# A hybrid attention and state-space encoder: attention steps that take two query heads of both key groups

## The chip, the cores and the metric

The kernel runs on one NeuronCore of a Trainium2 chip. The metric is the device time of one execution in microseconds (us), from the first to the last instruction and the little around them. The core has a matmul engine (PE, with its weight loads shown apart as PEld), a vector engine (DVE), a scalar engine (ACT), GpSimd (POOL) and a queue engine (SP) which here only starts transfers. Each runs its own list of instructions in order and waits for the others by semaphores. PE writes to eight banks of accumulators (`ps`), from which DVE and ACT read.

## The reference

Two sequences of 256 positions and 1024 channels go through two layers. Each layer projects its input once and splits the columns between windowed attention and a two-way state-space scan; the results are joined by an output projection, and a gated MLP follows. The change touches the attention alone:

```
q: 8 heads of 64, k and v: 2 groups of 64; heads 0-3 use group 0, heads 4-7 group 1
sc    = q_blk . k * HEAD_DIM**-0.5              # per block of 128 queries
mask  = (|q_pos - k_pos| <= 128) & in range
m     = max(max(sc), sink[head])
p     = exp(sc - m)
probs = p / (sum(p) + exp(sink[head] - m))
out   = probs . v                                # (block, head, 64)
```

All is computed in fp32 or by splitting a number into a high and a low part. There are 4 query blocks of 128 (`t`, two per sequence) and 8 heads, so 32 pairs of block and head in a layer.

## The kernel before

Both sequences lie side by side as 512 columns. A projection ("unit") streams 512 KB of weights from memory into a ring of five buffers; ACT takes the high part (`whi`, L545), DVE the low part (`wlo`, L1068), and PE makes 24 products of 128x512 per unit (L749, L750, L751). Units 0 to 26 of a layer are the input projection.

The order of all work is written out by hand in `mixer_schedule` (line 102) as one list of steps; every engine walks through it and does its own share of each step. For unit n it has `G` (the projection, PE), `E` (its first read, ACT), `F` and `F2` (a convolution of five taps on DVE, L1177), `SILU` (ACT, then DVE L1184), `S` (the split of the weights four units ahead). Attention is woven in from unit 8 on, one attention step i with each unit: `AS` (scores, PE), `AM` (row maxima, DVE L1322 to L1325), `AX` (four exponentials, ACT L682), `AD` (denominators, DVE), `AN` (division, POOL L494), `AP` (eight transposes of the probabilities on PE, L1007, and a copy by ACT, L691), `AV` (values, PE L1016; the result's high part by ACT L696, its low part by DVE L1338). `AP` of step i comes one unit after its scores and `AV` two units after. Besides there are `T` (transposes for the scan, L916), `CB` (L924), `MV` (POOL L524), and from unit 17 on the steps of the scan, among them `SB` (L957, L961) and `SD` (L977).

There are eight attention steps i per layer. `ATTN` (line 85) says what each holds: block t and key group g, that is, four heads of one block. The keys and values of group 0 lie in rows 0 to 63 of their buffers, those of group 1 in rows 64 to 127; the query buffer `qk[:, j]` holds head j of group 0 in its upper half and head j of group 1 in its lower half. So a step works with one half of the rows:

- `AS` writes banks 2 and 3. For each bank: a mask (L993, one product of the whole array), then two score products (L997) of 64 rows, all from rows g*64 to g*64+63.
- `AV` writes rows g*64 to g*64+63 of one bank by two products of 64 columns x 512 (L1016), one per block of keys.

An fp32 product shows as two records of PE in the trace, each with its weight load; a product of operands declared fp32r (the masks, the projections) shows as one.

The waits that matter here: the scores of step i wait for the exponentials of step i-1 (`as_exp`); DVE's `AM` waits for the scores (`as_full`); the transposes wait for POOL's division (`as_norm`); projection n waits until the convolution of unit n-2 has read its bank (`conv_taps`). The steps `AA` (L894, L895) and `SD` (L977) of before already put out into the two halves of a bank's rows in turn.

Of the kernel before, what the change touches and what calls it, by code (L numbers as in the profile page):

```python
# [19 lines left out]
ALU = mybir.AluOpType  # L20
# [4 lines left out]
P = 128  # L25
DEPTH, D_MODEL, SEQ, NSEQ = 2, 1024, 256, 2
TOK = NSEQ * SEQ
BLK = 128
# [53 lines left out]
PAIRS = [(g, t) for g in range(2) for t in range(NBLK)]  # L82
PRODS = [(i, kind) for i in range(len(PAIRS)) for kind in ("fwd", "bwd", "off")]
CN_HEAD = CN["upper"][0]
ATTN = [(t, g) for t in range(NBLK) for g in range(2)]
A0 = 8
PROD_SLOTS = {17: [0], 18: [1, 2], 19: [3, 4, 5], 20: [6, 7, 8], 21: [9, 10, 11], 22: [12, 13, 14],
              23: [15, 16, 17], 24: [18, 19, 20], 25: [21, 22], 26: [23]}
# [90 lines left out]
def trunk(nc, x_in, units, pm_d, pf_d, cn_d, gb_d, h_d, y_d):  # L179
    ctx = ExitStack()  # L180
    with ctx:
# [173 lines left out]
        def aux_bank(key):  # L355
            return 6 + aux_use[key] % 2
# [181 lines left out]
        def _(act):  # L538
# [61 lines left out]
            for L in range(DEPTH):  # L600
                act.wait_ge(pm_loaded, L * 16 + 16)
                for what, i in SCHED:
# [38 lines left out]
                    elif what == "SP":  # L641
                        act.wait_ge(dt_abs, L + 1)
                        A(sp[:, 2, :], sp[:, 1, :], ACT.Exp, scale=-1.0).then_inc(dt_exp, 1)
                        A(neg_a[:], pmc("a_log"), ACT.Exp).then_inc(dt_exp, 1)
                        act.wait_ge(dt_floor, L + 1)
                        A(sp[:, 2, :], sp[:, 4, :], ACT.Ln).then_inc(dt_log, 1)
                    elif what == "SM":
                        wait_aux_full(act, L, ("AA", 0))
                        A(own_hi[:], ps[:, aux_bank(("AA", 0)), :], ACT.Copy).then_inc(own_high, 1)
                        wait_aux_full(act, L, ("AO", 0))  # L650
                        for d in range(2):
                            rows = slice(d * 64, d * 64 + 64)
                            src = ps[rows, aux_bank(("AO", 0)), :].rearrange("p (a b s) -> p a b s", b=2, s=P)[:, :, d, :]
                            A(off_hi[rows, :, :], src, ACT.Copy).then_inc(off_high, 1)
                    elif what == "T":
                        wait_aux_full(act, L, ("T", i))
                        A(xs_tm[:, :, (i - 4) * P:(i - 3) * P], ps[:, aux_bank(("T", i)), :].rearrange("p (t c) -> p t c", c=P),
                          ACT.Copy, scale=0.5).then_inc(t_evac, 1)
                    elif what == "VT":
                        wait_aux_full(act, L, ("VT", 0))  # L660
                        A(v_tm[:], ps[:, aux_bank(("VT", 0)), :].rearrange("p (t c) -> p t c", c=P),
                          ACT.Copy).then_inc(v_done, 1)
                    elif what == "SE":
                        i, kind = PRODS[i]
                        k = 3 * i + ("fwd", "bwd", "off").index(kind)
                        act.wait_ge(seg_full, L * 24 + k + 1)
                        if kind == "bwd":
                            if i >= 1:
                                act.wait_ge(w_sum, L * 8 + i)
                        elif i >= 2:  # L670
                            wait_aux_full(act, L, ("SD", i - 2))
                        dst = {"fwd": e_fwd[i % 2], "bwd": e_bwd, "off": e_off[i % 2]}[kind]
                        b0 = 2 + 2 * (k % 2)
                        A(dst[:].rearrange("p h q -> p (h q)"),  # L674
                          ps[:, b0:b0 + 2, :].rearrange("p b n -> p (b n)"), ACT.Exp).then_inc(exp_done, 1)
                    elif what == "AX":
                        act.wait_ge(as_max, L * 8 + i + 1)
                        if i >= 2:

                            wait_y_full(act, L, ("AP", i - 2, 1))  # L680
                        for j in range(QPK):
                            A(sc[i % 2][:, j, :], ps[:, 2 + j // 2, (j % 2) * SEQ:(j % 2 + 1) * SEQ], ACT.Exp, scale=SCALE,  # L682
                              bias=ast[:, i % 2, 1, j:j + 1], accum_out=ast[:, i % 2, 3, j:j + 1])
                        A(ast[:, i % 2, 4, :], ast[:, i % 2, 2, :], ACT.Exp).then_inc(as_exp, 1)
                    elif what == "AP":
                        wait_y_full(act, L, ("AP", i, 1))
                        if i >= 2:
                            wait_aux_full(act, L, ("AV", i - 2))

                        assert y_bank(("AP", i, 0)) == 4  # L690
                        A(p_t[i % 2][:], ps[:, 4:6, :], ACT.Copy).then_inc(pt_done, 1)  # L691
                    elif what == "AV":
                        t, g = ATTN[i]
                        rows = slice(g * HEAD, (g + 1) * HEAD)
                        wait_aux_full(act, L, ("AV", i))
                        A(ahi[rows, 0:QPK, t * BLK:(t + 1) * BLK],  # L696
                          ps[rows, aux_bank(("AV", i)), :].rearrange("p (j q) -> p j q", q=BLK),
                          ACT.Copy).then_inc(ah_done, 1)
                    elif what == "SQ":
                        act.wait_ge(gated, L * 8 + (4 if i < 4 else 8))  # L700
                        if i >= 4:

                            act.wait_ge(rms_pair, L * 4 + 3)
                        A(sqr[i % 4][:], zs[:, i, :], ACT.Square).then_inc(rms_sq, 1)
                    elif what == "RMS":
                        act.wait_ge(rms_mm, L + 1)
                        A(std[:], ps[:, aux_bank(("RS", 0)), :], ACT.Sqrt, bias=cst("eps")).then_inc(rms_std, 1)
                    elif what == "RN":
                        act.wait_ge(ssd_normed, L * CT + i + 1)
                        A(ahi[:, QPK + i, :], zs[:, i, :], ACT.Copy).then_inc(sh_done, 1)  # L710
# [33 lines left out]
        def _(pe):  # L744
# [85 lines left out]
            for L in range(DEPTH):  # L830
                for what, i in SCHED:
# [147 lines left out]
                                              start=own, stop=not own, skip_group_check=True)  # L979
                        last.then_inc(aux_full, 1)  # L980
                    elif what == "AS":
                        t, g = ATTN[i]
                        rows = slice(g * HEAD, (g + 1) * HEAD)
                        if i == 0:
                            pe.wait_ge(rope_done, L * 5 + 5)
                            pe.wait_ge(as_const, 3)
# [1 line left out]

                            pe.wait_ge(as_exp, L * 8 + i)
                        o = 1 - t % 2  # L990
                        for m in range(2):

                            mm(ps[:, 2 + m, :].rearrange("p (j k) -> p j k", k=SEQ)[:, :, o * P:(o + 1) * P], big_i[:],  # L993
                               cut[:, t % 2, :].unsqueeze(1).broadcast_to((P, 2, P)), start=True, stop=False,
                               skip_group_check=True)
                            for n in range(2):
                                last = mm(ps[:, 2 + m, n * SEQ:(n + 1) * SEQ],  # L997
                                          qk[rows, 2 * m + n, t * BLK:(t + 1) * BLK],
                                          qk[rows, 4, (t // 2) * SEQ:(t // 2 + 1) * SEQ], start=False, stop=True,
                                          skip_group_check=True)  # L1000
# [7 lines left out]
                                                           sc[i % 2][:, j, kt * P:(kt + 1) * P], ident)  # L1008
                            last.then_inc(y_full, 1)
                    elif what == "AV":  # L1010
                        t, g = ATTN[i]
                        pe.wait_ge(v_done, L + 1)
                        pe.wait_ge(pt_done, L * 8 + i + 1)
                        wait_aux_free(pe, L, (what, i))
                        for kt in range(2):
                            last = mm(ps[g * HEAD:(g + 1) * HEAD, aux_bank((what, i)), :],  # L1016
                                      v_tm[:, (t // 2) * 2 + kt, g * HEAD:(g + 1) * HEAD], p_t[i % 2][:, kt, :],
                                      start=(kt == 0), stop=(kt == 1))
                        last.then_inc(aux_full, 1)
                    elif what == "RS":  # L1020

# [39 lines left out]
        def _(dve):  # L1061
# [99 lines left out]
            for L in range(DEPTH):  # L1161
                dve.wait_ge(pm_loaded, L * 16 + 16)
                for what, i in SCHED:
# [151 lines left out]
                        V.scalar_tensor_tensor(out=z, in0=y, scalar=0.5, in1=z, op0=ALU.mult, op1=ALU.mult).then_inc(gated, 1)  # L1315
                    elif what == "AM":

                        t, g = ATTN[i]
                        dve.wait_ge(as_full, L * 8 + i + 1)
                        sink = pmc("sink", g * QPK, (g + 1) * QPK)  # L1320
                        top, minus, sink_in = (ast[:, i % 2, n, :] for n in range(3))
                        chain(V.tensor_reduce(top, ps[:, 2:4, :].rearrange("p b (j k) -> p (b j) k", k=SEQ), AX_X, ALU.max))  # L1322
                        chain(V.scalar_tensor_tensor(out=top, in0=top, scalar=SCALE, in1=sink, op0=ALU.mult, op1=ALU.max))
# [8 lines left out]
                        chain(V.tensor_tensor(den, ast[:, i % 2, 3, :], ast[:, i % 2, 4, :], ALU.add))  # L1332
                        V.reciprocal(den, den).then_inc(as_den, 1)
                    elif what == "AV":
                        t, g = ATTN[i]
                        rows = slice(g * HEAD, (g + 1) * HEAD)
                        dve.wait_ge(ah_done, L * 8 + i + 1)
                        V.tensor_tensor(alo[rows, 0:QPK, t * BLK:(t + 1) * BLK],  # L1338
                                        ps[rows, aux_bank((what, i)), :].rearrange("p (j q) -> p j q", q=BLK),
                                        f(ahi[rows, 0:QPK, t * BLK:(t + 1) * BLK]), ALU.subtract).then_inc(al_done, 1)  # L1340
                    elif what == "RMS":
                        dve.wait_ge(rms_std, L + 1)
                        chain(V.reciprocal(std[:], std[:]))
# [78 lines left out]
def lay_out(x_prompt, x_sample, ln_in_g, ln_in_b, w_in, attn_sink, ssd_conv_w, ssd_conv_b, ssd_a_log,  # L1422
# [23 lines left out]
    for i in range(DEPTH):  # L1446
# [15 lines left out]
        cbias = np.concatenate([ssd_conv_b[i][SSD_WIDTH:], ssd_conv_b[i][:SSD_WIDTH]])  # L1462
        pms.append(np.concatenate([
            cw.reshape(5, N_CONV, P).transpose(2, 1, 0).reshape(P, 5 * N_CONV), channels(cbias),
            channels(ssd_norm_g[i]), everywhere(attn_sink[i]), everywhere(ssd_a_log[i]),
            everywhere(ssd_dt_bias[i]), channels(np.repeat(ssd_d[i], HEAD))], axis=1))
        pfs.append(np.concatenate([
            ffn_conv_w[i].reshape(3, FT, P).transpose(2, 1, 0).reshape(P, 3 * FT), channels(ffn_conv_b[i]),
# [26 lines left out]
```

## Time and profile before

| | |
|---|---|
| median of 3 runs | 1448.69 us (1447.71 to 1449.17) |
| the profiled execution | 1446.43 us, its span 1444.6 us |
| mean granted clock of PE | 0.991 |
| busy, share of the span: PE | 1393.3 us, 96% |
| PE weight loads | 1112.7 us, 77% |
| DVE | 767.1 us, 53% |
| ACT | 564.5 us, 39% |
| POOL | 194.3 us, 13% |
| score products (L997), 128 records | 36.1 us busy |
| value products (L1016), 64 records | 30.9 us busy |
| masks of the scores (L993), 32 records | 10.6 us busy |

Times of instructions are durations, and successive matmuls overlap in them: what a matmul costs PE is the distance from its start to the start of the next one. A granted clock of 1.00 is 2.4 GHz, one of 0.50 is 1.2 GHz.

### The profile page before, as it was taken

How to read it: one execution, taken by the hardware profiler on the slowest of the kernel's cores; microseconds unless marked ns; L12 is line 12 of the kernel's file. 1: busy time of each engine (PE TensorE's matmuls, PEld its weight loads, DVE VectorE, ACT ScalarE, POOL GpSimd, SP SyncE). 2: the span in 40 equal slices, each digit the busy share in tenths (PEclk: the TensorE clock that was granted, in tenths of full speed). 3: DMA queues.
4: the chain of work that ended last, by engine and by line, in shares of the span. 5: the costliest groups of instructions: out<-in, count | busy, mean ns of one | idle time of the engine just before them, and what ended most of it. 6: DMA issues, size and time to landing. Idle time of an engine off the chain costs nothing.

```text
span 1444.6 us, 16237 instructions
## 1 busy us (share of the span) xinstructions
PE 1393.3 (96%) x6676; PEld 1112.7 (77%) x6676; DVE 767.1 (53%) x1008; ACT 564.5 (39%) x849; POOL 194.3 (13%) x111
## 2 busy tenths in 40 slices
PE   6999999999999999999989999899989999999997
PEld 5776777777888888888777767677878888888885
DVE  5666675665544444432266767665655444443224
ACT  5445544343533333311253454534344333332112
POOL 1012320133100000060020124001610000001400
PEclk8999999999999999999999999999999999999999
DMA  3421111142232333333233211111413333333332
GB/s 154 147 72 45 44 45 58 45 175 88 73 102 93 97 102 90 100 121 98 73 91 133 59 44 44 59 44 59 177 56 117 91 99 102 89 101 122 97 90 100
DMA packets 33209, 129.93 MB, mean 90 GB/s; under 512 B 3728, under 2 KB 3888, under 8 KB 31984
## 3 DMA queue, kind: packets, MB, share of 16 engines
q1 hardware_dynamic: 32976, 128.61, 27.9%
q8 instruction: 53, 0.87, 0.3%
q0 software_dynamic: 160, 0.29, 0.1%
q14 instruction: 20, 0.16, 0.0%
HBM read 122.60 MB, written 6.29 MB: 89 GB/s over the span
## 4 chain that ended last, share of the span: by engine, by line
PE 85%; ACT 6%; DVE 4%; issue 2%; DMA 1%; POOL 0%; DVEq 0%; ACTq 0%
PE ps L749 17%; PE ps L750 17%; PE ps L751 17%; PE ps L792 7%; PE ps L793 7%; PE ps L794 7%; PE ps L997 2%; PE ps L1016 2%; PE ps L977 2%; ACT junk L550 2%; DVE hb L1083 1%; PE ps L1007 1%; ACT whi L545 1%; ACT e_fwd L674 1%; DVE cv L1177 1%
## 5 line engine op out<-in xcount | busy, mean ns | idle before, releaser
L749 PE MATMUL ps<-hhi,whi 128*128 128x512 f32 (+1 forms) x1200 | 466.4, 389 | 16.3 <-DVE hlo L1114 15.3
L750 PE MATMUL ps<-hlo,whi 128*128 128x512 f32 (+1 forms) x1200 | 455.8, 380 | 0.0
L751 PE MATMUL ps<-hhi,wlo 128*128 128x512 f32 (+1 forms) x1200 | 455.7, 380 | 0.0
L1068 DVE TENSOR_TENSOR wlo<-raw,whi 128x1024 fp32r<-128x1024 f32 x210 | 274.4, 1307 | 266.8 <-ACT whi L545 266.7
L545 ACT ACTIVATE whi<-raw 128x1024 fp32r<-128x1024 f32 x210 | 221.3, 1054 | 240.4 <-DMA raw<-in_units 240.1
L749 PEld LDWEIGHTS ps<-hhi,whi 128*128 128x128 f32 x1200 | 228.0, 190 | 66.2 <-issue 16.8
L750 PEld LDWEIGHTS ps<-hlo,whi 128*128 128x128 f32 x1200 | 228.2, 190 | 42.6 <-issue 2.4
L751 PEld LDWEIGHTS ps<-hhi,wlo 128*128 128x128 f32 x1200 | 228.0, 190 | 42.6
L792 PE MATMUL ps<-whi,uhi 128*128 128x512 f32 x352 | 139.4, 396 | 0.0
L794 PE MATMUL ps<-wlo,uhi 128*128 128x512 f32 x352 | 139.2, 396 | 0.0
L793 PE MATMUL ps<-whi,ulo 128*128 128x512 f32 x352 | 139.2, 396 | 0.0
L1363 DVE SCALAR_TENSOR_TENSOR gcv<-ps,pf,gcv 128x510 f32<-128x510 f32 x44 | 33.0, 749 | 158.9 <-ACT gcv L721 158.9
L721 ACT ACTIVATE gcv<-ps,pf 128x512 f32<-128x512 f32 x44 | 34.2, 777 | 171.7 <-PE ps L751 171.7
L471 POOL TENSOR_TENSOR hb<-hb,gb 128x1024 f32<-128x1024 f32 x8 | 20.9, 2646 | 498.9 <-DMA gb<-in_gb 498.9
L792 PE MATMUL ps<-whi,ahi 128*128 128x512 f32 x192 | 77.7, 404 | 2.5 <-DVE wlo L1068 2.4
L794 PEld LDWEIGHTS ps<-wlo,uhi 128*128 128x128 f32 x352 | 66.2, 188 | 16.0
L792 PEld LDWEIGHTS ps<-whi,uhi 128*128 128x128 f32 x352 | 66.2, 188 | 15.9
L793 PEld LDWEIGHTS ps<-whi,ulo 128*128 128x128 f32 x352 | 66.2, 188 | 15.8
L793 PE MATMUL ps<-whi,alo 128*128 128x512 f32 x192 | 76.0, 396 | 0.0
L794 PE MATMUL ps<-wlo,ahi 128*128 128x512 f32 x192 | 75.9, 396 | 0.0
L1373 DVE TENSOR_TENSOR guf<-gsg,ps 128x512 f32<-128x512 f32 x44 | 30.2, 687 | 83.0 <-PE ps L751 82.4
L1177 DVE SCALAR_TENSOR_TENSOR cv<-ps,pm,cv 128x508 f32<-128x508 f32 (+1 forms) x96 | 71.4, 744 | 2.8
(168 smaller groups left out, 1466.6 us busy)
## 6 DMA issues: line engine op xcount, KB each, us to landing
raw<-in_units SPq DMA_DIRECT2D x210, 512.0 KB, 3.6
gb<-in_gb SPq DMA_DIRECT2D x5, 1024.0 KB, 5.7
h_kept<-hb SPq DMA_DIRECT2D x2, 2048.0 KB, 9.3
ha<-h_kept SPq DMA_DIRECT2D x2, 2048.0 KB, 10.6
hb<-in_x SPq DMA_DIRECT2D x4, 512.0 KB, 6.2
out_y<-hb SPq DMA_DIRECT2D x4, 512.0 KB, 2.6
cn<-in_cn SPq DMA_DIRECT2D x1, 585.5 KB, 9.7
pm<-in_pm POOLq DMA_DIRECT2D x2, 80.0 KB, 3.4
```

The lines of the kernel that those rows point to most:

```text
L545: A(whi[:, m % RING, :], raw[:, m % RING, :], ACT.Copy).then_inc(unit_hi, 1)
L721: A(gcv[:], ps[:, bank, :], ACT.Identity, scale=pf[:, k * 3 + w0 + 1:k * 3 + w0 + 2], bias=pf[:, k + v0:k + v0 + 1]).then_inc(glu_center, 1)
L749: mm(out, whi[:, slot, cols], xhi, start=start, stop=False)
L750: mm(out, whi[:, slot, cols], xlo, start=False, stop=False)
L751: return mm(out, wlo[:, slot, cols], xhi, start=False, stop=stop)
L792: mm(ps[:, bank, :], xhi[:, rows], whi[:, slot, cols], start=start, stop=False)
L793: mm(ps[:, bank, :], xlo[:, rows], whi[:, slot, cols], start=False, stop=False)
L794: return mm(ps[:, bank, :], xhi[:, rows], wlo[:, slot, cols], start=False, stop=stop)
L1068: V.tensor_tensor(wlo[:, m % RING, :], raw[:, m % RING, :], f(whi[:, m % RING, :]), ALU.subtract).then_inc(unit_split, 1)
L1177: V.scalar_tensor_tensor(out=dst[:, :, lo:hi], in0=src[:, :, lo + s:hi + s], scalar=pmc("conv_w", 5 * j + tap, 5 * j + tap + 1), in1=dst[: ...
L1363: V.scalar_tensor_tensor(out=dst[:, :, 1:SEQ], in0=src[:, :, 0:SEQ - 1], scalar=pf[:, k * 3 + w0:k * 3 + w0 + 1], in1=dst[:, :, 1:SEQ], op ...
L1373: V.tensor_tensor(guf[:], gsg[:], ps[:, bank + 1, :], ALU.mult).then_inc(glu_done, 1)
```

## The change

`ATTN` now pairs a block t with a number m of 0 or 1. A step holds heads 2m and 2m+1 of group 0 and heads 2m and 2m+1 of group 1 of one block: still four heads. Bank 2 takes group 0's two heads, bank 3 group 1's. In `AS` both masks come first, and then four score products, whose rows alternate between the upper and the lower half. In `AV` each of two blocks of keys gives one product per group, of 64 columns x 256, whose output alternates between the upper and the lower half of one bank. ACT's and DVE's reads of that bank (L696 and L1338 before) now take 128 partitions x 256 in place of 64 x 512. The sink logits are sorted to match.

```
-ATTN = [(t, g) for t in range(NBLK) for g in range(2)]
+ATTN = [(t, m) for t in range(NBLK) for m in range(2)]
...
                     elif what == "AS":
-                        for m in range(2):
+                        for g in range(2):
-                            mm(ps[:, 2 + m, :].rearrange(...)[:, :, o * P:(o + 1) * P], big_i[:], cut...)
+                            mm(ps[:, 2 + g, :].rearrange(...)[:, :, o * P:(o + 1) * P], big_i[:], cut...)
-                            for n in range(2):
-                                last = mm(ps[:, 2 + m, n * SEQ:(n + 1) * SEQ],
+                        for n in range(2):
+                            for g in range(2):
+                                rows = slice(g * HEAD, (g + 1) * HEAD)
+                                last = mm(ps[:, 2 + g, n * SEQ:(n + 1) * SEQ],
                                           qk[rows, 2 * m + n, t * BLK:(t + 1) * BLK],
                                           qk[rows, 4, (t // 2) * SEQ:(t // 2 + 1) * SEQ], start=False, stop=True,
                                           skip_group_check=True)
...
                     elif what == "AV":
                         for kt in range(2):
-                            last = mm(ps[g * HEAD:(g + 1) * HEAD, aux_bank((what, i)), :],
-                                      v_tm[:, (t // 2) * 2 + kt, g * HEAD:(g + 1) * HEAD], p_t[i % 2][:, kt, :],
-                                      start=(kt == 0), stop=(kt == 1))
+                            for g in range(2):
+                                last = mm(ps[g * HEAD:(g + 1) * HEAD, aux_bank((what, i)), 0:2 * BLK],
+                                          v_tm[:, (t // 2) * 2 + kt, g * HEAD:(g + 1) * HEAD],
+                                          p_t[i % 2][:, kt, g * 2 * BLK:(g + 1) * 2 * BLK],
+                                          start=(kt == 0), stop=(kt == 1), skip_group_check=True)
...
-                        A(ahi[rows, 0:QPK, t * BLK:(t + 1) * BLK],
-                          ps[rows, aux_bank(("AV", i)), :].rearrange("p (j q) -> p j q", q=BLK),
+                        A(ahi[:, 2 * m:2 * m + 2, t * BLK:(t + 1) * BLK],
+                          ps[:, aux_bank(("AV", i)), 0:2 * BLK].rearrange("p (j q) -> p j q", q=BLK),
...
-                        V.tensor_tensor(alo[rows, 0:QPK, t * BLK:(t + 1) * BLK],
+                        V.tensor_tensor(alo[:, 2 * m:2 * m + 2, t * BLK:(t + 1) * BLK],
...
-            channels(ssd_norm_g[i]), everywhere(attn_sink[i]), everywhere(ssd_a_log[i]),
+            channels(ssd_norm_g[i]), everywhere(attn_sink[i].reshape(2, 2, 2).transpose(1, 0, 2)), everywhere(ssd_a_log[i]),
```

PE's instructions in the third attention step of a layer, before: the last product of the projection, the scores, the values and the transposes of two earlier steps, and the next projection's first product (`p_t` is the transposed probabilities, `sc` the probabilities).

```order
L751 MATMUL ps<-hhi,wlo 128x512
L993 MATMUL ps<-cut,big_i 128x2x128
L997 MATMUL ps<-qk 128x256 x2
L993 MATMUL ps<-cut,big_i 128x2x128
L997 MATMUL ps<-qk 128x256 x2
L1016 MATMUL ps<-p_t_68,v_tm 64x512 x2
L1007 MATMUL ps<-cn,sc_67 128x128 x8
L749 MATMUL ps<-hhi,whi 128x512
```

The same place afterwards (line numbers of the changed kernel: L992 and L998 for L993 and L997, L1018 for L1016, L1008 for L1007).

```order
L751 MATMUL ps<-hhi,wlo 128x512
L992 MATMUL ps<-cut,big_i 128x2x128 x2
L998 MATMUL ps<-qk 128x256 x4
L1018 MATMUL ps<-p_t_68,v_tm 64x256 x4
L1008 MATMUL ps<-cn,sc_67 128x128 x8
L749 MATMUL ps<-hhi,whi 128x512
```

The masks have moved together in front of all score products, and two value products of 512 columns have become four of 256.

DVE's instructions of the same kind of step before, from the row maxima to the first denominator instruction:

```order
L1322 TENSOR_REDUCE ast<-ps 128x4
L1323 SCALAR_TENSOR_TENSOR ast<-ast,pm 128x4
L1324 TENSOR_SCALAR ast<-ast 128x4
L1325 TENSOR_TENSOR ast<-pm,ast 128x4
L1338 TENSOR_TENSOR alo<-ps,ahi 64x4x128
L1068 TENSOR_TENSOR wlo<-raw,whi 128x1024
L1177 SCALAR_TENSOR_TENSOR cv<-ps,pm,cv 128x2x254
L1177 SCALAR_TENSOR_TENSOR cv<-ps,pm,cv 128x2x255
L1332 TENSOR_TENSOR ast<-ast 128x4
```

And afterwards, where only the shape of the read of the values differs:

```order
L1325 TENSOR_REDUCE ast<-ps 128x4
L1326 SCALAR_TENSOR_TENSOR ast<-ast,pm 128x4
L1327 TENSOR_SCALAR ast<-ast 128x4
L1328 TENSOR_TENSOR ast<-pm,ast 128x4
L1340 TENSOR_TENSOR alo<-ps,ahi 128x2x128
L1071 TENSOR_TENSOR wlo<-raw,whi 128x1024
L1180 SCALAR_TENSOR_TENSOR cv<-ps,pm,cv 128x2x254
L1180 SCALAR_TENSOR_TENSOR cv<-ps,pm,cv 128x2x255
L1335 TENSOR_TENSOR ast<-ast 128x4
```

No instruction of DVE, ACT, POOL or SP has changed its place in its engine's list.

## Rows read from the trace of the kernel before

**Rows 1.** PE's waits: line, what it waited for, us, times, longest.

```profile
PE ps L749 <- DVE hlo L1114: 15.3, 9, 3.1
```

**Rows 2.** Busy time by engine, layers' attention stretches; then PE clock, DMA share, GB/s.

```profile
87.98:187.80 99.82, 99.68 (x430) 69.14 (x429) 69.29 (x120) 52.09 (x121) 30.22 (x18) 1.00 0.17 50
796.70:896.50 99.80, 99.65 (x430) 69.14 (x429) 69.28 (x120) 52.09 (x121) 30.21 (x18) 1.00 0.17 50
```

**Rows 3.** Time order, PE, first score step: start us, duration us, engine, line, operation.

```profile
87.98 0.28 PE L993 MATMUL ps<-cut,big_i 128*128 128x256 f32 x1
88.19 1.13 PE L997 MATMUL ps<-qk 64*128 64x256 f32 x4
...
88.51 0.81 PE L997 MATMUL ps<-qk 64*128 64x256 f32 x3
...
88.94 0.38 PE L997 MATMUL ps<-qk 64*128 64x256 f32 x1
89.25 0.38 PE L993 MATMUL ps<-cut,big_i 128*128 128x256 f32 x1
...
90.62 0.50 PE L749 MATMUL ps<-hhi,whi 128*128 128x512 f32 x1
```

**Rows 4.** Time order, PE, fp32r products of 256 columns.

```profile
33.55 0.28 PE L750 MATMUL ps<-hlo,whi 128*128 128x256 f32 x1
33.67 0.28 PE L751 MATMUL ps<-hhi,wlo 128*128 128x256 f32 x1
```

**Rows 5.** Time order, PE, first value step.

```profile
107.86 1.93 PE L1016 MATMUL ps<-p_t,v_tm 128*64 128x512 f32 x4
...
109.20 0.59 PE L1016 MATMUL ps<-p_t,v_tm 128*64 128x512 f32 x1
...
109.72 1.09 PE L1007 MATMUL ps<-cn,sc 128*128 128x128 f32 x8
```

**Rows 6.** Time order, PE, a state step that alternates column halves.

```profile
207.77 0.44 PE L977 MATMUL ps<-e_fwd,xs_tm 128*64 128x128 f32 x4 [0.20 <-DVE e_off L1296]
...
209.32 0.42 PE L977 MATMUL ps<-e_off,xs_tm 128*64 128x128 f32 x4
```

**Rows 7.** Time order, PE, cumulative sums; four records of L895 stand between.

```profile
54.08 0.44 PE L894 MATMUL ps<-cn,la_sides 128*64 128x128 f32 x4
...
54.51 0.44 PE L894 MATMUL ps<-cn,la_sides 128*64 128x128 f32 x4
```

**Rows 8.** Time order, DVE, POOL and PE, first three attention steps.

```profile
89.65 0.69 DVE L1184 SCALAR_TENSOR_TENSOR bc<-bc,cv 128x512 f32<-128x512 f32 x1 [0.70 <-ACT bc L640]
90.72 1.23 DVE L1322 TENSOR_REDUCE ast<-ps 128x4 f32<-128x1024 f32 x1 [0.38 <-PE ps L997]
...
97.54 0.69 DVE L1184 SCALAR_TENSOR_TENSOR bc<-bc,cv 128x512 f32<-128x512 f32 x1 [0.69 <-ACT bc L640]
...
95.56 1.89 POOL L494 TENSOR_TENSOR sc<-sc,ast 128x1024 f32<-128x1024 f32 x1 [58.08 <-DVE ast L1333]
...
96.19 0.28 PE L993 MATMUL ps<-cut,big_i 128*128 128x256 f32 x1
98.82 1.09 PE L1007 MATMUL ps<-cn,sc 128*128 128x128 f32 x8
...
105.22 0.28 PE L993 MATMUL ps<-cut,big_i 128*128 128x256 f32 x1
...
116.11 0.28 PE L993 MATMUL ps<-cut,big_i 128*128 128x256 f32 x1
```

**Rows 9.** Time order, DVE and PE, towards the end of the stretch.

```profile
175.94 2.25 DVE L1184 SCALAR_TENSOR_TENSOR xsc<-xsc,cv 128x512 f32<-128x512 f32 x1
...
179.81 0.60 PE L916 MATMUL ps<-cn,xsc 128*128 128x128 f32 x4
```

**Rows 10.** Busy time by engine, before and in a stretch of low clock.

```profile
355.00:359.40 4.40, 2.25 (x14) 1.64 (x13) 3.79 (x9) 1.95 (x4) 1.40 (x1) 1.00 0.67 236
359.50:362.80 3.30, 3.30 (x18) 3.30 (x17) 0.88 (x3) 3.27 (x8) 0.35 (x1) 0.50 0.00 0
```

More of the change, by code:

```diff
@@ L692, in _ @@
                     elif what == "AV":
-                        t, g = ATTN[i]
-                        rows = slice(g * HEAD, (g + 1) * HEAD)
+                        t, m = ATTN[i]
                         wait_aux_full(act, L, ("AV", i))
-                        A(ahi[rows, 0:QPK, t * BLK:(t + 1) * BLK],
-                          ps[rows, aux_bank(("AV", i)), :].rearrange("p (j q) -> p j q", q=BLK),
+                        A(ahi[:, 2 * m:2 * m + 2, t * BLK:(t + 1) * BLK],
+                          ps[:, aux_bank(("AV", i)), 0:2 * BLK].rearrange("p (j q) -> p j q", q=BLK),
                           ACT.Copy).then_inc(ah_done, 1)
@@ L981, in _ @@
                     elif what == "AS":
-                        t, g = ATTN[i]
-                        rows = slice(g * HEAD, (g + 1) * HEAD)
+                        t, m = ATTN[i]
                         if i == 0:
@@ L990, in _ @@
                         o = 1 - t % 2
-                        for m in range(2):
-                            mm(ps[:, 2 + m, :].rearrange("p (j k) -> p j k", k=SEQ)[:, :, o * P:(o + 1) * P], big_i[:],
+                        for g in range(2):
+                            mm(ps[:, 2 + g, :].rearrange("p (j k) -> p j k", k=SEQ)[:, :, o * P:(o + 1) * P], big_i[:],
                                cut[:, t % 2, :].unsqueeze(1).broadcast_to((P, 2, P)), start=True, stop=False,
                                skip_group_check=True)
-                            for n in range(2):
-                                last = mm(ps[:, 2 + m, n * SEQ:(n + 1) * SEQ],
+                        for n in range(2):
+                            for g in range(2):
+                                rows = slice(g * HEAD, (g + 1) * HEAD)
+                                last = mm(ps[:, 2 + g, n * SEQ:(n + 1) * SEQ],
                                           qk[rows, 2 * m + n, t * BLK:(t + 1) * BLK],
@@ L1010, in _ @@
                     elif what == "AV":
-                        t, g = ATTN[i]
+                        t, m = ATTN[i]
                         pe.wait_ge(v_done, L + 1)
@@ L1316, in _ @@
                     elif what == "AM":
-                        t, g = ATTN[i]
+                        t, m = ATTN[i]
                         dve.wait_ge(as_full, L * 8 + i + 1)
-                        sink = pmc("sink", g * QPK, (g + 1) * QPK)
+                        sink = pmc("sink", m * QPK, (m + 1) * QPK)
                         top, minus, sink_in = (ast[:, i % 2, n, :] for n in range(3))
@@ L1334, in _ @@
                     elif what == "AV":
-                        t, g = ATTN[i]
-                        rows = slice(g * HEAD, (g + 1) * HEAD)
+                        t, m = ATTN[i]
                         dve.wait_ge(ah_done, L * 8 + i + 1)
-                        V.tensor_tensor(alo[rows, 0:QPK, t * BLK:(t + 1) * BLK],
-                                        ps[rows, aux_bank((what, i)), :].rearrange("p (j q) -> p j q", q=BLK),
-                                        f(ahi[rows, 0:QPK, t * BLK:(t + 1) * BLK]), ALU.subtract).then_inc(al_done, 1)
+                        V.tensor_tensor(alo[:, 2 * m:2 * m + 2, t * BLK:(t + 1) * BLK],
+                                        ps[:, aux_bank((what, i)), 0:2 * BLK].rearrange("p (j q) -> p j q", q=BLK),
+                                        f(ahi[:, 2 * m:2 * m + 2, t * BLK:(t + 1) * BLK]), ALU.subtract).then_inc(al_done, 1)
                     elif what == "RMS":
```

## Prediction

> **What bounds the kernel now.** The first view is the list of what the matmul engine (PE) waited for. Its longest entry lies in the layer norms, 15.3 us [rows 1], and no line of the attention steps stands in it as a waiter. The second is the busy time in the two stretches that hold the attention steps, one per layer. PE is busy 99.68 of 99.82 us and 99.65 of 99.80 us at a granted clock of 1.00, the 2.4 GHz level; the vector engine (DVE) is busy 69.3 us, the scalar engine (ACT) 52.1 us and POOL 30.2 us [rows 2]. So PE sets the time there: what is taken from PE comes off the end, until one of the others is late. The third view is PE's instructions in order of time, which shows what one step costs PE.
>
> **Scores, before.** The steps of a score product are two masks (L993) and four products (L997). Each fp32 product stands as two records. From the first mask at 87.98 to the next projection at 90.62 the step takes 2.64 us [rows 3]. Inside it: mask to first score record 88.19 - 87.98 = 0.21. First to second record 88.51 - 88.19 = 0.32; then three records start from 88.51 to 88.94, so two gaps of 0.215, which I call a slot (256 columns of an fp32 product take two). Last record to the next mask 89.25 - 88.94 = 0.31. Two things are thus paid beside the slots. Going from a mask, which uses all 128 rows of the array, to a 64-row score, or back, costs about 0.1 us over what the instruction before it needs; and the first weight load behind such a change is open, 0.32 - 0.215 = 0.105. The step makes four such changes, the changed one makes two: both masks go first.
>
> **Scores, after.** Mask to mask costs one record of 256 columns in one pass, 33.67 - 33.55 = 0.12 [rows 4]. The four products become eight records, now four in the upper 64 rows and four in the lower. If the two halves run beside each other, each has four records: 0.12 + 0.21 + 0.32 + 2 x 0.215 + 0.31 = 1.39, and I add half a slot, 0.11, since the second half must load its weights behind the first. That makes 1.50 and saves 1.14 us a step. No row of before has two row halves in turn, so this is bounded from both sides. Low end: 1.39, no offset. If the halves run one after the other with their loads hidden, as now within one half, the eight records cost seven gaps: 0.12 + 0.21 + 0.32 + 6 x 0.215 + 0.31 = 2.25, saving 0.39. High end: every weight load open, 0.12 + 0.21 + 7 x 0.32 + 0.31 = 2.88, with the first one of the second half open as well 2.99, which would cost 0.35 more than now. I take 1.50, because the nearest rows, those of column halves below, show halves that run beside each other.
>
> **Values, before and after.** A value product (L1016) is two fp32 products of 512 columns, four records: 107.86 to the next engine use at 109.72 is 1.86 us [rows 5]. From the first start to the last is 109.20 - 107.86 = 1.34 = 0.05 + 3 x 0.43. Afterwards there are four products of 256 columns, of which two go to each column half. Here the trace has the answer: the state products (L977) write the two column halves in turn, and 28 records of 128 columns start between 207.77 and 209.32, 0.055 us each [rows 6]. A record of 128 columns alone takes half of the 0.215 that one of 256 takes [rows 3], 0.108. So alternating column halves double the rate, for fp32 too. The changed step is then 0.05 + 4 x 0.215 + (109.72 - 109.20 - 0.43 = 0.09) + 0.04 for an offset of the second half = 1.04, saving 0.82. Bounds: 0.86 without overheads, 1.86 if nothing overlaps.
>
> A second row tells how deep this overlap reaches. The cumulative sums of L894 and L895 are issued as L894, L895 for one column half, then L894, L895 for the other (lines 888 to 895). The trace groups them as four records of L894, then four of L895, the next four L894 0.43 us later [rows 7]: eight records of 128 columns in 0.43, and the other half's L894 has started before this half's L895. The halves run as two queues that do not wait for each other's order. The Trainium skill, "TensorE: Matmul & The Clock Gate" (What overlaps and what doesn't) says the opposite: matmuls start and end strictly in program order. By the skill's rule a half would have to wait for the second pass of the other; rows 7 speak against it. "TensorEngine Tiling (Array Packing)" of the Trainium skill (Key Properties) has tiles working independently of each other, and with that the trace agrees.
>
> **What becomes late.** The 16 steps of a layer's stretch (eight of scores, eight of values) save PE 8 x 1.14 + 8 x 0.82 = 15.7 us. DVE issues the same number of instructions in the same order; only L1338 and ACT's L696 change shape, from 64 partitions x 512 to 128 x 256, which cannot be longer, so I count nothing. DVE stays at 69.3 us of what would be 99.8 - 15.7 = 84.1, 82%. Its own load shows in the first step: from one silu (L1184) at 89.65 to the next at 97.54 are 7.89 us, of which 0.38 is a wait for the scores (L1322 at 90.72, its releaser L997): it needs 7.5. PE's first step now takes 96.19 - 87.98 = 8.21 and would take 7.07; the second 105.22 - 96.19 = 9.03, then 7.89; the third 116.11 - 105.22 = 10.89, then 8.94 [rows 8]. Only the first is shorter than DVE's. What is late is the first transpose of the probabilities (L1007 at 98.82). It needs POOL's product L494, 95.56 + 1.89 = 97.45, behind the reduction L1322. That one can only come forward to the end of the silu, 89.65 + 0.69 = 90.34, by 0.32 with the usual gap. So the product is ready at 97.13, while PE comes 2 x 1.14 earlier, at 96.54: 0.6 us of new wait. The same at the other end of the stretch: a silu that now takes 2.25 us beside POOL's work ends at 175.94 + 2.25 = 178.19, and PE transposes its result at 179.81 [rows 9]. The slack is 1.62, the two value steps in front of it give PE 1.62, and DVE gets part of that itself; I allow 0.3. Loss per layer 0.9.
>
> After the stretch PE's waits hang on chains that start with it and move with it: the state stage, the output projection, the loads (at most one of 512 KB per projection, as elsewhere), and POOL's affine work behind the reload. I let the gain through whole.
>
> **The sum.** Per layer 15.7 - 0.9 = 14.8, two layers 29.6 us. The profiled execution took 1446.43 us (span 1444.6 and 1.8 around it): 1416.8. The median of the runs stands 2.26 above it, so the forecast is 1448.69 - 29.6 = 1419.1 us.
>
> **Rivals.**
> 1. *Row halves do not overlap* (only the changes of mode are saved). For it: no row shows two row halves. Against: column halves do it, in fp32. Per layer 8 x 0.39 + 8 x 0.82 = 9.7, less 0.1: 19.2 us in all, 1429.5. Chance 0.13.
> 2. *Halves overlap only in program order*, so that the two records of a product stay behind each other and eight records take five slots instead of four. Against: rows 7. Scores 1.39 + 0.215 = 1.61, values 1.00 + 0.215 = 1.22, together 0.29 a step less, 16 times 4.6: 1423.7. The Trainium skill's rule on program order, named above, is this case. Chance 0.07.
> 3. *DVE and its chain become the bound* beyond the first step: each of the first four steps of a layer costs 1 us more than I count, as its waits for ACT (0.7 at each silu, [rows 8]) stop being covered. 8 us: 1427. Against: from the second step on PE's step is the longer one. Chance 0.06.
> 4. *Each row change opens a weight load*: scores 2.99 us, 0.35 x 16 = 5.6 dearer, values 13.1 cheaper, no new wait. 1441.2. Chance 0.04.
> 5. *Slower than before: the clock.* If PE's new waits in the attention steps bring its clock to 1.2 GHz, work there takes twice as long, so T us at the low level cost T/2. The trace has the low level at 359.5 to 362.8, granted 0.50, behind a stretch in which PE was busy 2.25 of 4.40 us [rows 10]. Slower needs 2 x 29.6 = 59 us of the 170 us of both stretches at that level; all of it would cost 85 us, 1504. Against: the waits I find are 0.6 and 0.3 us. Chance 0.03.
>
> **How the numbers follow.** The forecast has 0.67. Its own range is 1414 to 1424: the offset and the losses are worth 2 us either way, and a stretch of low clock in a layer norm (3.4 us, costing 1.7) may come or go as the work shifts, twice. The whole range reaches to rival 1 and over 2 and 3: 1413 to 1431, leaving out 4 and 5 and a bit of each. Changes under 0.2% (2.9 us) can't be told from none. Faster 0.96 (forecast and rivals 1 to 4), same 0.01, slower 0.03.
>
> **What would show it.** Right: the scores' records of the two halves start in pairs within one slot, first mask to next projection near 1.5 us; value steps near 1.04; attention stretches of 84 to 86 us with PE still over 98% busy; a wait of PE before the first transposes in each layer, released by POOL, near 0.6 us; the state stage as long as before. Wrong: score records at even gaps of 0.215 (rival 1) or five slots (2); PE waits of 1 us and more for DVE in many steps (3); gaps of 0.32 (4); granted clock under 1.00 in the stretches (5).

## The result, and the profile after

| | before | changed |
|---|---|---|
| median | 1448.21 us (4 runs, 1447.71 to 1449.17) | 1413.72 us (4 runs, 1412.00 to 1414.69) |
| ratio | | 0.976, 95% interval 0.9748 to 0.9772 |
| span of the profiled execution | 1444.6 us | 1410.2 us |

The change takes 34.5 us; 29.6 were forecast. The median lies inside the forecast's range of 1413 to 1431 us by only 0.7 us, and 0.3 us below the narrower range of its main case, 1414 to 1424.

The two attention stretches, as in [rows 2], in the same columns: span, busy time of PE, weight loads, DVE, ACT and POOL, granted clock.

```profile
87.95:171.01 83.06, 82.44 (x462) 64.03 (x460) 66.89 (x120) 50.28 (x121) 29.18 (x17) 1.00 0.20 58
779.20:862.20 83.00, 82.39 (x462) 64.02 (x460) 66.84 (x120) 50.28 (x121) 29.18 (x18) 1.00 0.20 58
```

Each stretch is 16.8 us shorter, PE is still busy in 99% of it at a granted clock of 1.00, and DVE now in 81%.

The first score step in PE's order of time, the counterpart of [rows 3]. The second fence is the same view cut to 50 ns: it keeps only the records that run in that moment.

```profile
87.95 0.39 PE L992 MATMUL ps<-cut,big_i 128*128 128x256 f32 x2
88.28 1.13 PE L998 MATMUL ps<-qk 64*128 64x256 f32 x8
89.34 0.50 PE L749 MATMUL ps<-hhi,whi 128*128 128x512 f32 x1
```

```profile
88.28 0.49 PE L998 MATMUL ps<-qk 64*128 64x256 f32 x2
```

Eight score records take the 1.13 us in which four stood before. Two records of 0.48 us begin at 88.28 and end together 0.49 us later: they start within 0.01 us of each other. The trace doesn't name the half of a record, but in the one-half kernel e3 below successive records start 0.215 us apart or more, so these two lie in different halves. The step is 89.34 - 87.95 = 1.39 us instead of 2.64, and it is that in 14 of 16 steps; the other two, one per layer, hold the wait below. The value step, counterpart of [rows 5]:

```profile
104.80 1.08 PE L1018 MATMUL ps<-p_t,v_tm 128*64 128x256 f32 x8
105.82 1.09 PE L1008 MATMUL ps<-cn,sc 128*128 128x128 f32 x8
```

It takes 1.02 us instead of 1.86. In the list of PE's waits one line is new, the first one below:

```profile
PE ps L1008 <- POOL sc L495: 1.2, 2, 0.6
...
PE ps L916 <- DVE xsc L1187: 0.4, 2, 0.2
```

The second has become smaller. Before, it was

```profile
PE ps L916 <- DVE xsc L1184: 1.3, 2, 0.7
```

Going through PE's groups of both traces one by one, from start to start, accounts for the rest. Per layer: eight score steps 8 x 1.25 = 10.0 us; eight value steps 8 x 0.85 = 6.8; the second score step holds a wait, -0.69; from L916 to L924 it is four times 0.16 less, 0.64; PE's wait before L916 in unit 18 is 0.65 before and 0.20 now, 0.45. That is 17.15 a layer and 34.3 in both, where the spans differ by 34.4. The groups between keep their length to 0.05 us, except in the layer norms: there single groups are up to 1.4 us longer or shorter, and these differences cancel to 0.1 us. Two profiles of the one changed kernel (after and a1) differ there in the same way, and by 1.6 us in one group of a state stage, so differences of this kind are not the change's.

### The profile page after: what moved, and what is told of

Its sections match the earlier page's. It is cut to its first block, busy times and chain, and to the rows that moved or that the text cites. A ratio compares the mean times of both kernels' runs of the same rounds, so it can differ in the third digit from the quotient of the medians.

```text
span 1410.2 us, 16365 instructions
## 1 busy us (share of the span) xinstructions
PE 1359.8 (96%) x6740; PEld 1103.2 (78%) x6740; DVE 757.5 (54%) x1008; ACT 560.0 (40%) x849; POOL 194.3 (14%) x111
## 4 chain that ended last, share of the span: by engine, by line
PE 83%; ACT 6%; DVE 6%; issue 3%; DMA 1%; POOL 1%; DVEq 0%; ACTq 0%; POOLq 0%
PE ps L749 17%; PE ps L751 17%; PE ps L750 17%; PE ps L792 8%; PE ps L793 7%; PE ps L794 7%; PE ps L977 2%; ACT junk L551 2%; DVE cv L1180 1%; DVE hb L1086 1%; PE ps L1008 1%; PE ps L1018 1%; ACT whi L546 1%; DVE wlo L1071 1%; ACT e_fwd L675 1%
## 5 line engine op out<-in xcount | busy, mean ns | idle before, releaser
L1071 DVE TENSOR_TENSOR wlo<-raw,whi 128x1024 fp32r<-128x1024 f32 x210 | 269.8, 1285 | 269.6 <-ACT whi L546 269.3
```

The costliest lines, as they stand in the source:

```text
L1071: V.tensor_tensor(wlo[:, m % RING, :], raw[:, m % RING, :], f(whi[:, m % RING, :]), ALU.subtract).then_inc(unit_split, 1)
```

## The experiments

Times are medians; the kernel before took 1448.13 us (1446.28 to 1449.22) beside e1, e3, e4 and e5, 1446.18 us (1445.4 to 1447.34) beside e2, e6 and e7, and 1447.86 us (1445.81 to 1449.47) beside e8, a1 and a2. The ratio to it is what compares across the groups. "Step" is the time from the first record of a score or value step to the next group of PE, as most of the 16 steps have it. e3 leaves out group 1's own queries and keys, e8 leaves out the second half of the array's columns, so neither computes group 1's attention.

| kernel | median us | ratio (95%) | score step | value step |
|---|---|---|---|---|
| e1, scores in blocks | 1411.97 | 0.9758 (0.9743 to 0.9772) | 1.39 | 1.02 |
| e2, values in blocks | 1412.90 | 0.9769 (0.9753 to 0.9786) | 1.39 | 1.02 |
| e3, one row half | 1425.09 | 0.9845 (0.9830 to 0.9860) | 2.25 | 1.02 |
| e4, before with masks first | 1441.74 | 0.9954 (0.9938 to 0.9971) | 2.25 | 1.86 |
| e5, masks between | 1430.89 | 0.9884 (0.9870 to 0.9899) | 2.64 | 1.02 |
| e6, reads by halves | 1418.09 | 0.9805 (0.9790 to 0.9820) | 1.39 | 1.02 |
| e7, division in two | 1411.79 | 0.9762 (0.9748 to 0.9777) | 1.39 | 1.02 |
| e8, one column half | 1425.51 | 0.9846 (0.9833 to 0.9860) | 1.39 | 1.87 |
| a1, changed kernel again | 1413.26 | 0.9760 (0.9746 to 0.9773) | 1.39 | 1.02 |
| a2, division in two again | 1412.77 | 0.9763 (0.9750 to 0.9776) | 1.39 | 1.02 |

### Does the overlap of row halves carry the score step? (e3, e8)

```
-                                rows = slice(g * HEAD, (g + 1) * HEAD)
+                                rows = slice(0, HEAD)
                                 last = mm(ps[:, 2 + g, n * SEQ:(n + 1) * SEQ],
```

> The changed kernel, but all four score products read the upper 64 rows (group 0's queries and keys), so the scores of group 1 are computed from the wrong operands; everything else stays. It takes the overlap of row halves away and leaves both masks first. If the overlap is what made the score step 1.39 us: step 1.39 + 4 x 0.215 = 2.25 us, +13.8 us in 16 steps, of which the wait of 0.69 us before the first transposes of each layer is given back: 1426. If fewer changes of mode explain the step: no change, 1413.7.

```profile
87.91 0.39 PE L992 MATMUL ps<-cut,big_i 128*128 128x256 f32 x2
88.23 1.99 PE L998 MATMUL ps<-qk 64*128 64x256 f32 x8
90.15 0.50 PE L749 MATMUL ps<-hhi,whi 128*128 128x512 f32 x1
```

In this order of time of e3 the same eight records take 1.99 us in one half where two halves need 1.13, and the step is 90.15 - 87.91 = 2.24 (2.25 in the table is the same by rounding). The wait before L1008 is gone from PE's list. The span is 1422.5 us, 12.3 above the changed kernel's; 16 x 0.86 - 2 x 0.69 = 12.4. The overlap theory holds, its rival (no change) falls. Row halves overlap fully, and that is worth 12.3 us, 13.7 in the steps less the 1.4 of the wait that it brings.

The same for the values:

```
-                                last = mm(ps[g * HEAD:(g + 1) * HEAD, aux_bank((what, i)), 0:2 * BLK],
+                                last = mm(ps[0:HEAD, aux_bank((what, i)), g * 2 * BLK:(g + 1) * 2 * BLK],
```

> The changed kernel, but all four value products go to the upper 64 columns of the array (group 1's result beside group 0's in the same rows of the bank), so that the reads take stale numbers for group 1; everything else stays. It takes the overlap of column halves away. If that overlap is the whole gain of the value step: 1.02 + 4 x 0.215 = 1.88 us a step, nothing given back, +13.8 us, about 1427.5. If shorter products of 256 columns explain part of it: less than 1.8 us a step.

```profile
104.80 1.94 PE L1018 MATMUL ps<-p_t,v_tm 128*64 128x256 f32 x8
106.67 1.09 PE L1008 MATMUL ps<-cn,sc 128*128 128x128 f32 x8
```

The value step is 106.67 - 104.80 = 1.87 us, what it was before with half as many products of twice the columns. So nothing of its gain comes from the shape of the products. The time is 1425.5 where about 1427.5 was expected. The steps give the expected 16 x 0.86 = 13.7; the span is 12.3 longer. 0.9 of the rest is read off the groups behind it: L916 to L924 became 0.04 us shorter and L924 to the next projection 0.07, eight times. In the changed kernel L924 starts as soon as its bank is free (see e6), and its second record starts 0.29 us after its first; in e8 PE comes later, the bank has been free for 0.42 us, and the second record follows after 0.22. So the wait for the bank still costs the changed kernel 0.11 us each time, 0.07 of it behind the wait. The layer norms, 0.7 us shorter in this profile, are the other part.

### Is it the alternation? (e1, e2)

The prediction called the halves two queues, from [rows 7]. These two kernels take the alternation away and leave the halves.

```
-                        for n in range(2):
-                            for g in range(2):
+                        for g in range(2):
+                            for n in range(2):
                                 rows = slice(g * HEAD, (g + 1) * HEAD)
```

> The changed kernel with the four score products in another order: both of group 0 first, then both of group 1, so that the row halves no longer alternate from product to product. If each half is a queue of its own, as the step of 1.39 us after the change suggests, the order doesn't matter: score step 1.39 us, time as the changed kernel, 1413.7 us. If halves overlap only in program order (the rule that matmuls start and end in order), just the last pass of group 0 lies beside the first of group 1: 7 slots of 0.215 instead of 4, step 2.04 us, 16 steps +10 us, 1424.

e2 has the same swap of loops, kt and g, in the value step.

> The changed kernel with the four value products in another order: both blocks of keys for group 0, then both for group 1. Independent column halves: value step 1.02 us as now, 1413.7 us. Overlap in program order only: 7 slots instead of 4, 1.66 us, 16 steps +10 us, 1424.

e1's score step, and then the same view cut to 150 ns at its start:

```profile
88.04 0.39 PE L992 MATMUL ps<-cut,big_i 128*128 128x256 f32 x2
88.36 1.14 PE L998 MATMUL ps<-qk 64*128 64x256 f32 x8
89.44 0.50 PE L749 MATMUL ps<-hhi,whi 128*128 128x512 f32 x1
```

```profile
88.36 0.49 PE L998 MATMUL ps<-qk 64*128 64x256 f32 x2
```

Two records start 0.01 us apart here too, so the first record of group 1 starts beside the first of group 0, although three other records of group 0 are issued ahead of it, and the step is 1.40 us. e2's value step is 1.02 us:

```profile
105.71 1.09 PE L1018 MATMUL ps<-p_t,v_tm 128*64 128x256 f32 x8
106.73 0.44 PE L1008 MATMUL ps<-cn,sc 128*128 128x128 f32 x2
```

Both times are that of the changed kernel within their intervals. Program order, which would have given steps of 2.04 and 1.66 us, is out. Both halves must merely be in one step; which comes first doesn't matter. In all these runs both halves hold the same amount of work, so that the record issued last also starts last; a step with unequal halves was not run. That speaks against the Trainium skill's sentence in "TensorE: Matmul & The Clock Gate" (What overlaps and what doesn't), that matmuls begin and end in program order; the rule of "TensorEngine Tiling (Array Packing)" (Key Properties), that tiles run independently, is what these runs show.

### What do the masks' places cost? (e4, e5)

e4 is the kernel before with the two masks in a loop of their own ahead of the products; e5 is the changed kernel with its masks back between them.

```
 e4:                    for m in range(2):
                            mm(ps[:, 2 + m, :]..., big_i[:], cut[...], start=True, stop=False, ...)
+                       for m in range(2):
                            for n in range(2):
                                last = mm(ps[:, 2 + m, ...], qk[rows, ...], qk[rows, 4, ...], ...)
 e5:                    for g in range(2):
                            mm(ps[:, 2 + g, :]..., big_i[:], cut[...], start=True, stop=False, ...)
-                       for n in range(2):
-                           for g in range(2):
+                           for n in range(2):
                                last = mm(ps[:, 2 + g, ...], qk[rows, ...], qk[rows, 4, ...], ...)
```

> The kernel before, with nothing changed but that both masks of a score step come ahead of its four products; groups and halves as before. Two of four changes between the whole array and 64 rows go: score step 2.64 - 0.39 = 2.25 us, 16 steps -6.2 us, 1442. If changes of mode cost nothing and only overlap pays: 1448.2.

> The changed kernel with the mask of bank 3 put back between group 0's two products and group 1's two, as the order of before was: mask, two, mask, two. If a product of the whole array between them drains both halves, nothing overlaps: score step 2.64 us as before, +20 us, less 1.4 for the first waits: 1432. If the halves could overlap across the mask: some 2.0 us a step, 1422.

e4's first score step, then e5's, in PE's order of time:

```profile
88.04 0.39 PE L992 MATMUL ps<-cut,big_i 128*128 128x256 f32 x2
88.36 1.99 PE L997 MATMUL ps<-qk 64*128 64x256 f32 x8
90.28 0.50 PE L749 MATMUL ps<-hhi,whi 128*128 128x512 f32 x1
```

```profile
87.93 0.28 PE L991 MATMUL ps<-cut,big_i 128*128 128x256 f32 x1
88.14 1.13 PE L996 MATMUL ps<-qk 64*128 64x256 f32 x4
89.19 0.38 PE L991 MATMUL ps<-cut,big_i 128*128 128x256 f32 x1
89.51 1.13 PE L996 MATMUL ps<-qk 64*128 64x256 f32 x4
90.57 0.50 PE L749 MATMUL ps<-hhi,whi 128*128 128x512 f32 x1
```

e4's step is 2.24 us, e5's 2.64, both as computed. e4 took 1441.7 us, 6.4 less than the kernel before, and 16 x 0.39 is 6.3: moving the masks is worth that much of the 34.5 by itself. In e5 the four records before the second mask are all in one half and the four behind it in the other; the mask needs all rows, and nothing passes it. e5 has both halves in one step, as the changed kernel, and gains nothing in its score step. So grouping both halves pays only for what stands on one side of a product of the whole array.

### Are the reads behind the values on PE's path? (e6)

In the result, two groups of PE that the change doesn't touch were shorter. My new theory: ACT's and DVE's reads of the values' bank are shorter (their forms in the traces: 0.59 and 0.68 us before, 0.38 and 0.42 now), and L924 waits for that bank.

```
-  A(ahi[:, 2 * m:2 * m + 2, ...], ps[:, aux_bank(("AV", i)), 0:2 * BLK]..., ACT.Copy).then_inc(ah_done, 1)
+  for g in range(2):
+      rows = slice(g * HEAD, (g + 1) * HEAD)
+      last = A(ahi[rows, 2 * m:2 * m + 2, ...], ps[rows, aux_bank(("AV", i)), 0:2 * BLK]..., ACT.Copy)
+  last.then_inc(ah_done, 1)
...                                   # DVE's subtraction in the same way
```

> The changed kernel, in which ACT and DVE read the values' bank in two instructions of 64 partitions x 256 each instead of one of 128 x 256. ACT's read then takes about 0.8 us instead of 0.38, DVE's 0.84 instead of 0.42. Theory: the shorter reads are on PE's path, since the products of L924 wait for the bank's release (al_done): four times per layer +0.8 us, and about 0.6 us once per layer in unit 18, where transposes wait for a chain behind these reads: +7.6 us, 1421. If the reads are covered, as I had counted: 1413.7.

PE and the reads in the fifth step's unit, first of the kernel before, then of the changed kernel, then of e6; DVE's read is the one that writes `alo`:

```profile
132.24 0.68 DVE L1338 TENSOR_TENSOR alo<-ps,ahi 64x512 fp32r<-64x512 f32 x1 [0.66 <-ACT ahi L696]
...
132.43 0.60 PE L916 MATMUL ps<-cn,xsc 128*128 128x128 f32 x4
133.06 1.10 PE L924 MATMUL ps<-bc 128*128 128x256 f32 x4
```

```profile
123.53 0.38 ACT L696 ACTIVATE ahi<-ps 128x256 fp32r<-128x256 f32 x1 [1.54 <-PE ps L1018]
...
124.26 0.42 DVE L1340 TENSOR_TENSOR alo<-ps,ahi 128x256 fp32r<-128x256 f32 x1
...
124.35 0.60 PE L916 MATMUL ps<-cn,xsc 128*128 128x128 f32 x4
124.82 1.10 PE L924 MATMUL ps<-bc 128*128 128x256 f32 x4
```

```profile
123.32 0.77 ACT L698 ACTIVATE ahi<-ps 64x256 fp32r<-64x256 f32 x2 [1.07 <-PE ps L1020]
...
124.12 0.86 DVE L1344 TENSOR_TENSOR alo<-ps,ahi 64x256 fp32r<-64x256 f32 x2
...
124.13 0.60 PE L918 MATMUL ps<-cn,xsc 128*128 128x128 f32 x4
125.12 1.10 PE L926 MATMUL ps<-bc 128*128 128x256 f32 x4 [0.39 <-DVE alo L1344]
```

From L916 to L924 are 0.63 us before, 0.47 in the changed kernel and 0.99 in e6. Before, DVE's read ends at 132.92 and L924 starts 0.14 later; the changed kernel's ends at 124.68, e6's at 124.98, and the product (L926 there) starts 0.14 and 0.15 later. The same distance, so this wait is on the path in all three. The waits before L916's transposes grew as well: PE's list of e6 has

```profile
PE ps L926 <- DVE alo L1344: 3.1, 8, 0.4
...
PE ps L918 <- DVE xsc L1189: 1.9, 4, 0.5
```

where the changed kernel has 0.4 us in two waits. Two of the four are those of unit 18, 0.5 where 0.2 was; the other two, 0.4 each, follow the layer's last value step, where the changed kernel has none. The theory holds: the reads are not covered. Its price was a little too high: by the ratios, 0.9805 - 0.9760 = 0.0045, it is 6.5 us where 7.6 were expected, and by PE's groups 8 x 0.51 + 2 x 0.31 + 2 x 0.51 = 5.7 (the median itself, 1418.1, was taken beside a kernel before that was 2 us faster there). Of the reads' 0.8 us more, only 0.52 arrives at L924. DVE's own 0.44 arrives whole. Of ACT's 0.39 only 0.08 does: in the changed kernel ACT's read ends at 123.91 and DVE, busy with its row maxima, starts its own at 124.26; in e6 ACT's ends at 124.09 and DVE's starts at 124.12.

### Can the new wait go? (e7, a1, a2)

```
-  nc.gpsimd.tensor_tensor(sc[i % 2][:], sc[i % 2][:], ast[...]..., ALU.mult).then_inc(as_norm, 1)
+  for kt in range(2):
+      part = sc[i % 2][:, :, kt * P:(kt + 1) * P]
+      nc.gpsimd.tensor_tensor(part, part, ast[...]..., ALU.mult).then_inc(as_norm, 1)
...
+  pe.wait_ge(as_norm, 2 * (L * 8 + i) + kt + 1)      # per key block in AP
```

> The changed kernel with POOL's division (L495) split into two instructions by key block, so that the first four transposes can start after the first half. Theory: the wait of PE for POOL before the first transposes (0.6 us, two times) goes, since the first half is ready some 0.95 us earlier and the second before the fourth transpose ends: -1.2 us, 1412.5. Rival: two instructions of 512 cost POOL clearly more than one of 1024 (1.9 us), and the second half comes later than the whole did: no gain or up to 1 us more.

The first transposes of the changed kernel and POOL's division, then both in a2, the same kernel as e7:

```profile
97.00 1.09 PE L1008 MATMUL ps<-cn,sc 128*128 128x128 f32 x8 [0.62 <-POOL sc L495]
...
95.05 1.89 POOL L495 TENSOR_TENSOR sc<-sc,ast 128x1024 f32<-128x1024 f32 x1 [57.61 <-DVE ast L1336]
```

```profile
96.30 0.66 PE L1009 MATMUL ps<-cn,sc 128*128 128x128 f32 x4
97.14 0.66 PE L1009 MATMUL ps<-cn,sc 128*128 128x128 f32 x4 [0.18 <-POOL sc L497]
...
95.05 2.04 POOL L497 TENSOR_TENSOR sc<-sc,ast 128x512 f32<-128x512 f32 x2 [57.61 <-DVE ast L1337]
```

The first four transposes start 0.70 us earlier, the other four wait for the second half, and two instructions cost POOL 0.15 us more than one. All eight take 1.25 us instead of 0.85, so the next projection starts at 97.55 instead of 97.85: 0.3 us won per layer, 0.6 in all, half of the 1.2 expected, because the second half comes later than the whole did (97.09 against 96.94), as the rival had it. The layer's last value step then takes 1.15 us instead of 1.02, and the wait in unit 18 is 0.13 shorter. e7 and the changed kernel had not run side by side, so both ran again on one chip.

> The changed kernel again, for the comparison with the split division on one chip: ratio 0.976 of the kernel before, two waits for POOL of 0.6 us.

> The changed kernel with POOL's division in two again, on the same chip as the changed kernel. Its first profile had a wait of 0.2 us where the changed kernel has 0.6 (twice); if nothing else hangs on it, 0.6 us (0.04%) less than the changed kernel, which the times can hardly tell from none; what the profiles differ in otherwise is the clock in the layer norms.

The ratios are 0.9760 (0.9746 to 0.9773) and 0.9763 (0.9750 to 0.9776). The profiles show the wait gone down, 1.3 to 0.4 us, and the times cannot tell the kernels apart. No version here is known to beat the changed kernel.

## Why the prediction was right, and where its terms were off

**What bounds the kernel** was right. PE was busy throughout the stretches and all that it gave up came off the end: 34.3 us by groups, 34.4 by the spans, 34.5 by the medians. The stretches are 83.1 us where 84 to 86 were named. Nothing became the bound behind it; DVE rose to 81% where 82% was worked out, though its busy time was held at 69.3 us and fell to 66.9. The gain was forecast a seventh too small, and the time is in the range by little: four of the five terms below were off in the same direction.

**Masks first**: 0.39 us a step, and 0.39 in e4.

**Row halves** ran beside each other as the nearest rows of column halves had suggested, and e3 shows it. The term was mis-sized by the half slot of 0.11 us that I added for the second half's weight load. The two first records start within 0.01 us, the step is 1.39, the low end of my bound: 16 x 0.11 = 1.8 us.

**Column halves**: 1.02 us for 1.04. The step fell by 0.85 where 0.82 was forecast, 0.5 us in all.

**The first wait**: 0.6 us forecast; PE waits 0.62 and the step is 0.69 longer, -0.2 us in all. Its place and its releaser, POOL's division, were right, and e7 moved it by splitting that instruction.

**The reads** were the step that failed: "which cannot be longer, so I count nothing". They became shorter, and e6 shows that PE waits for them. In [rows 2] and the list of waits this could not be seen: before, L924 started 0.63 us after L916 where 0.44 is enough (e8), and these 0.2 us stood in no line, being inside the overlap of matmul durations. It gave 8 x 0.16 = 1.3 us.

**The end of the stretch** went the other way: I allowed a loss of 0.3 us a layer before the transposes at 179.81 of [rows 9], and none came; in the changed kernel the silu ends 1.05 us before their counterpart starts. Instead PE gained 0.45 us a layer behind the stretch, in unit 18, where I had let the waits move along unchanged. The two make 1.5 us. This wait stood in the list of before, in the line of 1.3 us above. It ends a chain behind the last value step: ACT's read, its split of the next weights, DVE's part of the split, the convolution, the silu. ACT's read, first in the chain, is 0.21 us shorter; the split starts 0.1 us before the read has ended where it had started 0.02 behind it, which is 0.13 more, and the convolution 0.1 earlier in the same way. e6, which lengthens the reads, gives 0.31 back. Why the two later instructions start earlier was not taken apart.

The five sum to 1.8 + 0.5 - 0.2 + 1.3 + 1.5 = 4.9, the distance from 29.6 to 34.5, to the tenth or two that the rounding and the layer norms leave open. The time itself came out 5.4 us under 1419.1; the other 0.5 is the median of the kernel before, 1448.69 us in the forecast and 1448.21 beside the result.

**The rivals**: that row halves don't overlap falls by the 1.39 us step and by e3; overlap in program order by e1 and e2; DVE as the bound by the even steps of 1.39 and 1.02 us after the second; open weight loads and a low clock by the same steps and the granted 1.00 in both stretches.

## What to carry to other kernels

A product that fills half of the array's rows or columns leaves the other half free, and if the step before the next full product holds equal work for both halves, its products take half the time, in fp32 as well; the order within the step is of no account (e1, e2), but what stands on either side of a product of the whole array (here a mask) doesn't overlap (e5). Each change between the whole array and a half cost about 0.2 us here (e4 makes two fewer and saves 0.39), worth saving by itself. Where PE is busy at 99%, look also at what reads the banks that it reuses: a wait of 0.1 to 0.2 us was inside the durations and in no list, and only the distance from one start to the next showed it.

## What was not expected of the hardware

The records of two halves start 0.01 us apart even where three more records of the first half are issued between them (e1), and the second half's weight loads, 0.18 to 0.19 us each, add nothing to the step. The step is as long as one half alone would need: 0.86 us for four records of 256 columns, 1.72 when both halves' records share one (2.25 against 1.39 in e3, 1.87 against 1.02 in e8).
